# Hybrid decoder trunk on one core: dense stages moved between the attention heads

## The reference, cut to what matters

```python
z = rms(x) @ w_in                                   # all projections and the three gates
y_d = diff_attention(dq, dk, dv)                    # 4 heads, two softmaxes each
y_m = mla(c_q, c_kv, k_rope)                        # 8 heads, from a low-rank latent
y_c = b_gate * conv3(c_gate * xv)                   # short convolution, width 512
g = sigmoid(gates)
mixed = g[0]*(y_d @ w_br_diff) + g[1]*(y_m @ w_br_mla) + g[2]*(y_c @ w_br_conv)
x = x + mixed @ w_out
x = x + peer(rms(x))                                # 8 heads x 16 experts out of 16384 for each token
x = x + sigmoid(rms(x) @ w_ple_gate) * (p @ w_ple_proj)
```

## Time and profile before

| | us |
|---|---|
| median of 3 runs | 3864.2 (3863.8 to 3873.48) |
| the profiled execution | 3872.2 |
| its span, first to last instruction | 3870.3 |
| busy: PE, PEld, DVE, ACT, POOL | 2969.0, 1519.9, 2583.5, 1446.0, 1367.3 |
| idle POOL waiting for DVE, for PE to free a slot | 936.7, 927.4 |
| mean granted clock of TensorE | 0.88 |

### The profile page before, as it was taken

One profiled execution on the slowest core, in us unless ns is written; L12 is line 12 of the kernel. 1 busy time (PEld: TensorE's weight loads), 2 busy tenths in 40 slices (PEclk: granted clock), 3 DMA queues, 4 the chain that ended last, 5 costly groups with the idle time before them and its releaser, 6 DMA issues. The chain is left out here.

```text
span 3870.3 us, 28848 instructions
## 1 busy us (share of the span) xinstructions
PE 2969.0 (77%) x8168; PEld 1519.9 (39%) x8168; DVE 2583.5 (67%) x5233; ACT 1446.0 (37%) x3974; POOL 1367.3 (35%) x1033
## 2 busy tenths in 40 slices
PE   8599759667998789766998779767998776555556
PEld 5354615334445335323446335334445432111112
DVE  1411587776666987775667987766666987777774
ACT  1320222557423343548323343547433242222222
POOL 0000033333333344444333444333332445555551
PEclk9779979888999899888999889888999988777778
DMA  4114379888998999989998999878998999999994
GB/s 167 61 69 159 115 302 388 312 330 335 365 390 335 363 366 415 405 355 356 391 385 341 394 374 414 338 304 335 360 389 347 372 371 415 422 422 422 422 421 196
DMA packets 182400, 1298.67 MB, mean 336 GB/s; under 512 B 20320, under 2 KB 21856, under 8 KB 26592
## 3 DMA queue, kind: packets, MB, share of 16 engines
q0 software_dynamic: 147456, 1073.81, 69.2%
q1 hardware_dynamic: 34784, 223.01, 14.6%
HBM read 1294.64 MB, written 2.10 MB: 335 GB/s over the span
## 5 line engine op out<-in xcount | busy, mean ns | idle before, releaser
L489 POOL DMA_INDIRECT ring<-in_uv,experts x1024 | 1364.8, 1333 | 2431.7 <-DVE x L1159 936.7
L1274 PE MATMUL ps_sum<-ring,diag 128*128 128x512 f32 x2144 | 1274.0, 739 | 742.3 <-ACT diag L731 735.4
L1150 DVE SCALAR_TENSOR_TENSOR ring<-ring,h_ffn 128x1024 f32<-128x1024 f32 x1024 | 1231.4, 1219 | 191.4 <-DMA ring<-in_uv,experts 185.3
L1274 PEld LDWEIGHTS ps_sum<-ring,diag 128*128 128x128 f32 x2144 | 454.2, 227 | 1438.0 <-ACT diag L731 1012.7
L723 ACT ACTIVATE dots<-dots 128x1 f32<-128x1 f32 x1024 | 205.6, 201 | 1502.3 <-DVE ring L1150 1500.9
L1159 DVE SCALAR_TENSOR_TENSOR x<-ring,weight,x 128x1024 f32<-128x1024 f32 x488 | 625.2, 1281 | 191.3 <-ACT weight L725 191.2
L1336 PE MATMUL ps_act<-wt,area_h 128*128 128x512 f32 (+1 forms) x1536 | 661.7, 590 | 2.5 <-ACT area_h L505 2.5
L1336 PEld LDWEIGHTS ps_act<-wt,area_h 128*128 128x128 f32 x1536 | 293.7, 192 | 362.1 <-issue 357.7
L1380 PE MATMUL ps_act<-area_h,wt 128*128 128x256 f32 x1536 | 347.4, 387 | 4.9 <-ACT area_h L505 4.9
L1380 PEld LDWEIGHTS ps_act<-area_h,wt 128*128 128x128 f32 x1536 | 297.1, 194 | 57.1 <-issue 9.1
L725 ACT ACTIVATE weight<-dots,gate 128x1 f32<-128x1 f32 x1024 | 301.6, 295 | 33.3
(11 more groups left out here) (173 smaller groups left out, 2072.0 us busy)
## 6 DMA issues: line engine op xcount, KB each, us to landing
wt<-in_weights SPq DMA_DIRECT2D x192, 1024.0 KB, 8.5
ring<-in_uv,experts POOLq DMA_INDIRECT x1024, 10.8
wt<-in_weights SPq DMA_DIRECT2D x12, 512.0 KB, 9.2
wt<-in_weights SPq DMA_DIRECT2D x4, 768.0 KB, 8.5
x<-in_x SPq DMA_DIRECT2D x4, 512.0 KB, 5.0
area_y<-in_keys SPq DMA_DIRECT2D x4, 512.0 KB, 8.1
area_f<-in_keys SPq DMA_DIRECT2D x4, 512.0 KB, 9.7
area_f<-in_ffn_rows SPq DMA_DIRECT2D x4, 512.0 KB, 4.4
```

The lines of the kernel that those rows point to most:

```text
L489: pool.indirect_dma_start(ring[:, row.slot, :], None, a[f"uv{row.step // 2}"][:, :], bass.IndirectOffsetOnAxis(ap=experts[:, row.step % 2, ...
L1150: dve.scalar_tensor_tensor(u, u, 1.0, h_ffn[:, row.tile, :], ALU.mult, ALU.mult, accum_out=dots[:, row.j:row.j + 1]).then_inc(dots_ready, 1)
L1274: ins = pe.matmul(ps_sum[:, b, :], diag[:, row.pe_before % DIAGS, :], ring[:, row.slot, D + b * 512:D + (b + 1) * 512], start=row.pe_first ...
```

## The change

**Places.** The convolution stages, `taps` and `latent` leave their places ahead of the diff attention. `attention` takes a list `between` and puts one of its stages at the end of each round from round 1 on. For the diff attention the list is the six convolution stages, `taps`, `latent`.

**Gates in two halves.** A mix pair becomes three stages: `gate_a` (tile 0), `gate_b` (tile 1) and a branch, 8 products of 128x512 each. The four pairs of branches 0 and 2, twelve stages, go between the mla heads, in rounds 1 to 12 of 19. The two pairs of branch 1, which needs the mla result, stay behind it.

**Buffers.** The gates lie in parts of `area_b` and `area_e` that the attentions don't use then. The weight tiles are stored in the new order of use.

**Rows.** `ROWS_IN` is changed. With it and with the new order, the rows dealt to stages change as follows, for steps 0, 1, 2:

| stages | rows before | after |
|---|---|---|
| convolution, taps, latent and diff attention | 41, 42, 42 | 34, 35, 35 |
| mla attention and mix | 67, 68, 68 | 66, 67, 67 |
| of these in the two last pairs | 9, 9, 9 | 14, 14, 14 |
| rows of the whole kernel that PE adds | 536 | 510 |

```diff
-    "diff_sq": 1, "diff_norm": 1, "diff_turn": 1.5, "diff_scores": 1.2, "diff_flip": 1.2, "diff_pv": 0.6, "diff_sub": 2,
-    "mla_norm": 5, "mla_up": 5, "mla_sums": 4, "mla_qk": 3, "mla_rope": 4, "mla_turn": 4, "mla_scores": 1, "mla_flip": 0.8,
-    "mla_pv": 0.5, "mla_out": 1.5, "mix_first": 5, "mix_more": 5, "mix_turn": 2, "out": 3.5,
+    "diff_sq": 1, "diff_norm": 1, "diff_turn": 1.5, "diff_scores": 0.8, "diff_flip": 0.8, "diff_pv": 0.4, "diff_sub": 2,
...
+    "mla_pv": 0.3, "mla_out": 1.5, "gate_a": 2.2, "gate_b": 2.2, "branch_first": 2.2, "branch_more": 2.2, "mix_turn": 2,
...
+MIX_EARLY, MIX_LATE = [(0, 0), (0, 2), (1, 0), (1, 2)], [(0, 1), (1, 1)]
...
+def attention(kind, d, heads, between):
...
+        if i >= 1 and between:
+            out.append(between.pop(0))
+    return out + between
...
+        out += attention("diff", d, DH, [("conv_c", d, 0), ("conv_c", d, 1), ("conv_x", d, 0), ("conv_x", d, 1),
+                                         ("conv_b", d, 0), ("conv_b", d, 1), ("taps", d), ("latent", d)])
...
+        out += attention("mla", d, MH, mix(d, MIX_EARLY))
         out += [("mla_out", d, t) for t in range(2)]
+        out += mix(d, MIX_LATE)
...
+            def gate_half(d, t):
+
+                bank = act_bank()
+                for kh in range(2):
+                    w = tile(kh).rearrange("p (k n) -> p k n", k=4)
+                    for k in range(4):
+                        ins = pe.matmul(bank, hT[:, 4 * kh + k, t * P:(t + 1) * P], w[:, k, :],
+                                        start=(kh + k == 0), stop=(kh == 1 and k == 3))
+                    if kh == 0:
+                        if t:
+                            ins.then_inc(w_used, 1)
```

More of the change, by code:

```diff
@@ L132, in choice, with mix @@
     return [("topk", d, t, part) for part in range(len(TOPK_OPS))]
-def attention(kind, d, heads):
-    out, n = [], 2 * heads
+def mix(d, pairs):
+    out = []
+    for n, br in pairs:
+        out += [("gate_a", d, n, br), ("gate_b", d, n, br), ("branch_more" if br else "branch_first", d, n, br)]
+    return out
+MIX_EARLY, MIX_LATE = [(0, 0), (0, 2), (1, 0), (1, 2)], [(0, 1), (1, 1)]
+MIX_SHARED = [(n, br) for n, br in MIX_EARLY + MIX_LATE if br != 1]
+def attention(kind, d, heads, between):
+    out, n, between = [], 2 * heads, list(between)
     for i in range(n + 3):
@@ L1518, in mix @@
                     tick()
-                release(3)
+                release(1)
             def mix_turn(at, d):
@@ L1592, in _layer_weights @@
     first = 1536 + LATENT
+    for n in range(3):
+        by_rows(w_in[:, 0:1536], n)
     for part in (1, 2, 0):
@@ L1597, in _layer_weights @@
         put(cut[0, 1])
-    for n in range(3):
-        by_rows(w_in[:, 0:1536], n)
     lat = np.zeros((D, 512), np.float32)
```

102 lines of the change are left out of this document (55 added, 47 removed).

## The result

The changed kernel takes 3890.7 us (median of 4 runs, 3887.5 to 3900.7), the kernel before 3864.0: a ratio of 1.0067, with an interval of 1.0047 to 1.0087. That is inside the range, but the forecast was 3864. The profiled execution took 3887.5 us; its span of 3885.7 is 15.4 longer than that of before.

What follows compares the result with a forecast made beforehand. No one engine bounds the kernel; the row standing in the flip and the DMA floor matter. Terms 1 - 11 - 35 - 6 + 52 = +1 on the profiled 3872.2 us; on the median 3864, 8-in-10 range 3805 to 3915.

Steps and rivals of the forecast that it cites:

- the term of -11: Mla attention and mix of step -1: gates between heads keep PE at 2.4 GHz, worth -11 us, bounds -15 and -3.

Runs made afterwards that it cites:

- e1: The changed kernel with only the convolution stages between the heads, the gate pairs back behind the mla heads: 3884.9 us.
- e3: The changed kernel with no stages between the heads, its shares of rows, split gates and buffers kept: 3879.6 us.
- e9: The kernel before with the sigmoid of the mix replaced by a plain copy that needs no table load: 3862.2 us.
- e11: The kernel before with none of the mla attention's rows on PE and 0.45 of those of the mix: 3863.0 us.
- e12: The changed kernel with no stages between heads, PE_PART 0 for mla stages and 0.45 for gates and branches: 3855.4 us.
- e4: The changed kernel in its order, with the old row weights for attention, gates and branches, and 2 for convolution and taps: 3982.3 us.
- e7: The changed kernel with PE_PART 0 for the mla stages and 0.45 for gates and branches: 3799.4 us.
- e14: The changed kernel with diff rounds' stage behind scores, PE_PART 0 for both attentions, 0.45 for gates, branches and convolution: 3727.5 us.
- e16: The changed kernel with PE_PART 0.45 for gates and branches and still 2/3 for the mla stages: 3880.2 us.

## What to carry to other kernels

When work is put between the links of a pipeline across in-order engines, adding up each engine's busy time in a round isn't enough: follow, for each instruction that another engine waits for, what now stands ahead of it in its own queue, and when that can start. Here the covering stages were worth nothing until the expert rows that need a fresh diagonal from ACT were taken from behind the flips (-91 to -121 us), and in the diff rounds the place of the stage, ahead of the wait that it should cover, was worth 29 to 58 more. Weigh an extra table load by whether somebody waits behind it, not by ACT's load.

## What was not expected of the hardware

The same stretch of the same instructions can get quite different clocks from one kernel to the next. The mla heads of step -1, without rows or stages between them, are the same in the kernel before, e1, e3, e9, e11 and e12: before took 32.5 us at a granted clock of 0.53 (fourth of the earlier trace rows), as did e1; e9 took 27.9 at 0.76 and e11 28.3 at 0.71. e3:

```profile
205.90:233.80 27.90, 24.14 (x114) 18.64 (x115) 9.45 (x64) 18.13 (x68) 0.00 (x0) 0.76 0.00 1
```

and e12:

```profile
203.00:235.20 32.20, 29.30 (x114) 23.64 (x115) 9.46 (x64) 18.21 (x68) 0.00 (x0) 0.55 0.00 1
```

All of step -1 took 508.1 us before and 501.6 in e11, which issues the same instructions there. So a comparison of two profiles can be off by 5 to 7 us in this step alone. Each kernel was profiled once, so it stays open whether this differs from one execution to the next or from one kernel to the next. If it is the execution, it may be most of the 8.2 by which the profiled one of before exceeds its median. It is about half of what the term of -11 was to win. The Trainium skill (TensorE: Matmul & The Clock Gate, "What's actually happening") says that the number of a kernel's first matmuls at the lower clock varies between runs; here it is a stretch at 205 us. With gates between the heads the stretch of heads and covered pairs stood at 0.96 in the change and in e4 to e7 and e14 to e16, and mla with mix took 153 to 154 us each time. The placement makes this stretch steady rather than faster than its best.
